# RWKV-7 time mixing in chunks: masks, sums of squares and the order of TensorE rearranged

## The reference

```python
kk = heads(k * p['k_k'])
kk = kk / jnp.maximum(jnp.sqrt(jnp.sum(kk * kk, axis=-1, keepdims=True)), 1e-12)
def step(S, inp):
    r_t, w_t, k_t, v_t, kk_t, b_t = inp            # b = kk * a
    sa = jnp.einsum('bhvk,bhk->bhv', S, -kk_t)
    S = (S * w_t[:, :, None, :] + sa[..., None] * b_t[:, :, None, :]
         + v_t[..., None] * k_t[:, :, None, :])
    o = jnp.einsum('bhvk,bhk->bhv', S, r_t)
    return S, o
mu = jnp.mean(o, axis=-1, keepdims=True)
var = jnp.mean(jnp.square(o - mu), axis=-1, keepdims=True)
o = ((o - mu) * lax.rsqrt(var + LNX_EPS)).reshape(B, L, W) * p['lnx_w'] + p['lnx_b']
```

## Time and profile before

| | |
|---|---|
| median of 3 runs | 2921.92 us (2918.57 to 2924.86) |
| the profiled execution | 2917.37 us |
| its span, first to last instruction | 2915.5 us |
| mean granted clock of TensorE | 0.936 of full |
| RWKV stage, first load to last output | about 1267 to 1793 us |
| a full turn in it (mean of six) | 59.4 us |

### The profile page before, as it was taken

The page is one execution under the profiler, slowest core; times in us unless marked ns, Lnnn a source line. Parts: engine busy times, 40 slices in busy tenths (PEclk is TensorE's granted clock), DMA queues, the critical chain, the costliest instruction groups (busy, mean ns, idle before and its releaser), DMA issues. The chain is left out here.

```text
span 2915.5 us, 48363 instructions
## 1 busy us (share of the span) xinstructions
PE 2679.0 (92%) x20914; PEld 2596.0 (89%) x20914; DVE 1137.0 (39%) x1650; ACT 428.8 (15%) x770; POOL 896.7 (31%) x445
## 2 busy tenths in 40 slices
PE   7999999999899999948899995489989999999997
PEld 7999999999899989947777774379989999999997
DVE  5834826522344554124344442554142122122224
ACT  3100000000200001023444331120031000000011
POOL 3434434343333422300000000154334343434432
PEclk9999999999999999968899886589999999999998
DMA  3111211111334252230001000124111111111111
GB/s 119 42 52 58 74 56 58 54 61 40 109 118 100 81 163 73 90 107 14 18 18 34 6 6 25 51 87 157 61 37 47 47 50 39 49 51 36 58 37 72
DMA packets 81408, 178.88 MB, mean 61 GB/s; under 512 B 11824, under 2 KB 39088, under 8 KB 80128
## 3 DMA queue, kind: packets, MB, share of 16 engines
q1 hardware_dynamic: 59200, 133.65, 14.8%
q10 hardware_dynamic: 22080, 43.36, 4.6%
HBM read 137.48 MB, written 38.33 MB: 60 GB/s over the span
## 5 line engine op out<-in xcount | busy, mean ns | idle before, releaser
L175 POOL TENSOR_TENSOR whi<-wraw,small 128x1024 fp32r<-128x1024 f32 (+3 forms) x214 | 361.3, 1688 | 1331.0 <-PE ps L209 1302.0
L209 PE MATMUL ps<-hhi,whi 128*128 128x344 f32 x3216 | 692.6, 325 | 73.1 <-DVE hhi L2367 24.2
L209 PE MATMUL ps<-hhi,wlo 128*128 128x344 f32 x3168 | 675.0, 322 | 0.0
L209 PE MATMUL ps<-hlo,whi 128*128 128x344 f32 x3120 | 667.2, 322 | 0.0
L209 PEld LDWEIGHTS ps<-hhi,whi 128*128 128x128 f32 x3216 | 547.4, 191 | 77.1 <-issue 55.5
L209 PEld LDWEIGHTS ps<-hhi,wlo 128*128 128x128 f32 x3168 | 534.0, 190 | 0.0
L209 PEld LDWEIGHTS ps<-hlo,whi 128*128 128x128 f32 x3120 | 533.1, 191 | 0.0
L178 POOL TENSOR_TENSOR wlo<-wraw,whi 128x1024 fp32r<-128x1024 f32 (+3 forms) x214 | 506.7, 2368 | 16.8
L209 PE MATMUL ps<-ahi,whi 128*128 128x344 f32 x1056 | 223.9, 320 | 0.0
L209 PE MATMUL ps<-alo,whi 128*128 128x344 f32 x1056 | 223.6, 320 | 0.0
L209 PE MATMUL ps<-ahi,wlo 128*128 128x344 f32 x1056 | 223.1, 319 | 0.0
(11 more groups left out here) (403 smaller groups left out, 2687.8 us busy)
## 6 DMA issues: line engine op xcount, KB each, us to landing
wraw<-ffn_up SPq DMA_DIRECT2D x88, 512.0 KB, 3.5
wraw<-ffn_down SPq DMA_DIRECT2D x32, 384.0 KB, 3.1
wraw<-ffn_down SPq DMA_DIRECT2D x32, 320.0 KB, 2.8
wraw<-w_mix SPq DMA_DIRECT2D x18, 512.0 KB, 3.6
gates<-gate_out ACTq DMA_DIRECT2D x16, 516.0 KB, 2.7
gates_in<-gates SPq DMA_DIRECT2D x16, 516.0 KB, 4.5
wraw<-w_gates SPq DMA_DIRECT2D x16, 512.0 KB, 3.5
f_mixed<-fmix ACTq DMA_DIRECT2D x14, 516.0 KB, 3.7
```

The source lines that it names most:

```text
L175: pool.tensor_tensor(g.whi[:, s, 0:n], g.wraw[:, s, 0:n], g.zero.to_broadcast([P, n]), ALU.add).then_inc(g.w_hi, 1)
L209: last = pe.matmul(g.ps[:, 3 * bank_set + b, 0:BLK], w[:, s, k * P:(k + 1) * P], x(k, b), start=(k == 0 and first), stop=(k == kt - 1 and ...
```

## The change

Masks become predicated copies (`copy_predicated`: where the mask is nonzero, the value is copied, elsewhere the destination keeps what it has). The destinations are prepared once: `X` gets five buffers, one per level, set to zero, and a new `T0` holds identities, which `first` overwrites in its masked places. The product of the identity in `level_x` goes away. `X` then holds only the part off the diagonal, and VectorE adds each level's product to T (`level_sum`), where ScalarE copied the product before. The signs move: `B` is stored negated, and two copies of ScalarE lose their factor -1. `join` on ScalarE uses a buffer of its own, `XJ`.

The sums of squares are turned round: `sums` multiplies a table of 16 selecting columns (weights 128x16) by the squares as moving data (128 columns), for the keys and the outputs together, eight products into one 16x128 result. VectorE scales it and runs the square root on 16 rows by 128 columns; `turned` and ScalarE's copy go away, and `key_scale` and `out_scale` read VectorE's result.

The order on TensorE and VectorE changes as the diff shows: `sums` stands behind `level_x` 3, `gate` behind `level_t` 2, `decayed` behind level 5, `decay_sum` between the sum of level 1 and the mask of level 2, `norms` between the mask and the sum of level 3. On ScalarE the bias of the bonus moves behind `sa`.

```diff
-    g.X, o = g.at("rw_x", o, [P, 2, 4, N])
+    g.X, o = g.at("rw_x", o, [P, 5, 2, 4, N])
...
-            def level(c, j):
-
-                for n in range(2):
-                    inv["pe"].wait(act, c, f"t{j}{n}")
-                    if j < 5:
-                        ins = act.activation(g.T2[:, n].rearrange("p x a c -> p (x a c)"), g.ps[:, 6 + n, :], ACT.Copy)
-                    else:
-                        act.activation(flat(g.T2[lo, n, 0]), g.ps[lo, 6 + n, 0:4 * N], ACT.Copy)
-                        for r in (lo, hi):
-                            ins = act.activation(g.TTF[r, c % 2, 4 * n:4 * n + 4, r], half(6 + n, 1)[r], ACT.Copy)
-                    q_ev.on(ins, f"t{j}{n}")
...
-            st.did(v.tensor_copy(g.identr[:, :], g.ident[:, :]))
-            st.do(v.tensor_copy(g.eyes[:, :].rearrange("p (a c) -> p a c", a=4),
-                                g.rtab[:, T_IST, 0:N].unsqueeze(1).to_broadcast([P, 4, N])))
+            for j in range(5):
+                st.did(v.memset(g.X[:, j], 0.0))
+            st.do(v.tensor_copy(g.T0[:, :, :, :, :].rearrange("p n x a c -> p (n x a) c"), eye(16)))
...
-            def key_norms(d):
-
-                pre["pe"].wait(v, d, "norms")
-                st.do(v.tensor_scalar(g.rsx[:, 0, 0:8], g.ps[:, 0, 0:8], 1e-24, None, ALU.max))
-                p_ev.mark(v, "norms")
...
-                tt(g.B[:, :, :], EA[:, :, :], EX[:, :, :], ALU.mult)
+                st.do(v.scalar_tensor_tensor(g.B[:, :, :], EA[:, :, :], -1.0, EX[:, :, :], ALU.mult, ALU.mult))
...
-                    tt(g.T2[:, n], g.ps[:, 6 + n, :].rearrange("p (x a c) -> p x a c", x=2, a=4), mask0, ALU.mult)
-                    t = g.T2[:, n].rearrange("p x a c -> p (x a) c")
-                    tt(t, t, eye8, ALU.add)
+                    st.do(v.copy_predicated(g.T0[:, n], mask0,
+                                            g.ps[:, 6 + n, :].rearrange("p (x a c) -> p x a c", x=2, a=4)))
                     q_ev.mark(v, f"m{n}")
 
             def level(c, j):
                 for n in range(2):
                     inv["pe"].wait(v, c, f"x{j}{n}")
-                    tt(g.X[:, n], half(4 + n, 0), mask(j), ALU.mult)
+                    st.do(v.copy_predicated(g.X[:, j - 1, n], mask(j), half(4 + n, 0)))
                     q_ev.mark(v, f"x{j}{n}")
+
+            def level_sum(c, j):
+                T = g.T0 if j == 1 else g.T2
+                for n in range(2):
+                    inv["pe"].wait(v, c, f"t{j}{n}")
+                    if j < 5:
+                        tt(g.T2[:, n].rearrange("p x a c -> p (x a) c"), T[:, n].rearrange("p x a c -> p (x a) c"),
+                           bank(6 + n, 8), ALU.add)
+                    else:
+                        tt(g.T2[lo, n, 0], g.T2[lo, n, 0], half(6 + n, 0)[lo], ALU.add, False)
+                        for r in (lo, hi):
+                            tt(g.TTF[r, c % 2, 4 * n:4 * n + 4, r], g.T2[r, n, 1], half(6 + n, 1)[r], ALU.add, r is hi)
+                    q_ev.mark(v, f"t{j}{n}")
...
-            def norms(k, s, p):
+            def norms(k):
                 x, y, t = (g.rsx[:, a, :] for a in range(3))
-                if s is not None:
-                    out["pe"].wait(v, s, "var")
-                    st.do(v.tensor_scalar(x[:, 8:16], g.ps[:, 3, 0:8], 1.0 / N, LNX_EPS, ALU.mult, ALU.add))
+                norm["pe"].wait(v, k, "sums")
+                st.do(v.tensor_scalar(x, g.ps[0:16, 3, CH:2 * CH], g.seg[0:16, 3:4], g.seg[0:16, 4:5], ALU.mult, ALU.add))
+                st.do(v.tensor_scalar(x, x, 1e-24, None, ALU.max))
                 rsqrt_steps(v, st, y, x, t)
                 n_ev.mark(v, "rs")
...
                     gated(y)
                 if q is not None:
-                    scores(q, 0)
-                    scores(q, 1)
-                if p is not None:
-                    key_norms(p)
-                if q is not None:
-                    scores(q, 2)
-                    scores(q, 3)
+                    for n in range(4):
+                        scores(q, n)
                     first(q)
                     level(q, 1)
                 if s is not None:
                     advance(s)
+                if q is not None:
+                    level_sum(q, 1)
                 if p is not None:
                     decay_sum(p)
                 if q is not None:
                     level(q, 2)
+                    level_sum(q, 2)
+                    level(q, 3)
                 if s is not None or p is not None:
-                    norms(k, s, p)
+                    norms(k)
                 if q is not None:
-                    level(q, 3)
+                    level_sum(q, 3)
                 if p is not None:
                     key(p)
                 if q is not None:
                     level(q, 4)
+                    level_sum(q, 4)
+                if p is not None:
+                    key_norm(p)
+                if q is not None:
+                    level(q, 5)
+                    level_sum(q, 5)
                 if p is not None:
                     decayed(p)
-                if q is not None:
-                    level(q, 5)
                 if s is not None:
...
             def level_x(c, j):
+                T = g.T0 if j == 1 else g.T2
                 for n in range(2):
-                    pe.matmul(g.ps[:, 4 + n, 0:4 * N], g.identr[:, :], g.eyes[:, :], start=True, stop=False)
                     if j == 1:
                         inv["dve"].wait(pe, c, f"m{n}")
                     else:
-                        inv["act"].wait(pe, c, f"t{j - 1}{n}")
+                        inv["dve"].wait(pe, c, f"t{j - 1}{n}")
                     for p in range(4):
                         for r in (lo, hi):
                             last = pe.matmul(g.ps[r, 4 + n, p * N:(p + 1) * N], g.SC[r, c % 2, 4 * n + p, 1, 0, r],
-                                             g.T2[r, n, 0, p, :], start=False, stop=p == 3)
+                                             T[r, n, 0, p, :], start=True, stop=True)
                     q_ev.on(last, f"x{j}{n}")
...
-            def var(i):
-                out["act"].wait(pe, i, "sq")
+            def sums(k, i, d):
+
+                use = []
+                if d is not None:
+                    pre["act"].wait(pe, d, "sq")
+                    use += [(p, SQ[:, p, :]) for p in range(4)]
+                if i is not None:
+                    out["act"].wait(pe, i, "sq")
+                    use += [(4 + p, g.osq[:, p, :]) for p in range(4)]
+                for n, (w, x) in enumerate(use):
+                    last = pe.matmul(g.ps[0:16, 3, CH:2 * CH], g.rtab[:, T_SUM, 16 * w:16 * w + 16], x,
+                                     start=n == 0, stop=n == len(use) - 1)
+                n_ev.on(last, "sums")
+
+            def out_scale(k, i):
...
                     tok(q)
                 if s is not None:
                     r0(s)
-                if p is not None:
-                    key_norms(p)
                 if q is not None:
                     scores(q, 0)
                     scores(q, 1)
@@ -1964,33 +1952,32 @@
                     o(s)
                 if q is not None:
                     level_x(q, 1)
-                if s is not None:
-                    centre(s)
                 if p is not None:
                     lora(p, 1)
                 if q is not None:
                     level_t(q, 1)
+                if s is not None:
+                    centre(s)
+                if q is not None:
                     level_x(q, 2)
+                    level_t(q, 2)
                 if p is not None:
                     gate(p)
-                if s is not None:
-                    var(s)
-                if q is not None:
-                    level_t(q, 2)
-                if s is not None or p is not None:
-                    turned(k)
                 if q is not None:
                     level_x(q, 3)
+                if s is not None or p is not None:
+                    sums(k, s, p)
+                if q is not None:
+                    level_t(q, 3)
+                    level_x(q, 4)
                 if p is not None:
                     key_scale(k, p)
                 if q is not None:
-                    level_t(q, 3)
+                    level_t(q, 4)
+                    level_x(q, 5)
                 if s is not None:
                     out_scale(k, s)
                 if q is not None:
-                    level_x(q, 4)
-                    level_t(q, 4)
-                    level_x(q, 5)
                     level_t(q, 5)
                     join(q)
```

129 lines of the change are left out of this document (57 added, 72 removed).

## The result

The changed kernel takes 2901.73 us (median of 4 runs, 2898.35 to 2906.01), the kernel before 2923.39 us beside it (4 runs, 2918.57 to 2926.18): ratio 0.9928, 95% interval 0.9909 to 0.9948. It is 0.7% or about 21 us faster. The forecast was 2925 us, slower or the same; the range began at 2904.

A forecast was written before the change was run, and what follows sets the result against it. TensorE, busy for 92% of the span, was taken as the bound, with its waits and half-clock time. Full turns 7 x -0.2, first turn +4.7 and last +0.9 gave +4 us on the 2921.92 median: about 2925 us, range 2904 to 2942.

The forecast's parts named there:

- The walk through the queues: Stepping through TensorE's and VectorE's queues in one full turn: new waits of 7.6 us against 4.75 before.
- The chain: VectorE's square root on 16x128: thirteen instructions, 3.9 us in place of 2.45, bounds 2.7 and 4.2.
- the first turn: Stage's first turn, where nothing hides `norms`: `tok` at 1308.2 in place of 1303.54, 4.7 us later.
- the rival that it reads twice: Predicated copies on VectorE take 0.69 and 1.22 us, masks stand open at every level: +5, 2930 us; chance 0.10.
- 10 x 0.31 = 3.1 us: TensorE time saved per full turn by dropping ten identity products in the levels, 0.31 us each.
- seven turns: The sum over the stage multiplied the per-turn change of -0.2 us by 7.
- The step on the clock: Change in a turn's half-clock loss: 0.5 us less at the moved stretch, 0 to 1.7 more around `join` and `tok`.
- 0.5 us less lost: Half-clock stretch moves from behind `gate` to behind the wait before `level_x` 4, covering 0.8 us of small waits.
- 0 to 1.7 us more lost: Longer idle around `join` and `tok` costs up to half of one more 3.4 us half-clock stretch per turn.
- the half-clock stretch goes with the wait: No clock fall follows the wait before `level_x` 4, or it is nearer 1.7 us: 2904 us; chance 0.27.

The follow-up runs named there:

- old_norms: Kernel after with the sums of squares and square root put back to 128 rows by 16 columns, in their new place; ratio 0.9881 to the kernel before.
- no_eye_gate_late: Kernel before without the identity products, `gate` and `var` behind `level_t` 2 and `turned` behind `level_x` 3; 2887.7 us, ratio 0.9887.
- r0_old_norms: Kernel after with queues reordered (`sums` behind `level_t` 2, `bonus` before `join`, `r0` before `tok`) and square root back in 128x16; 2864.1 us, ratio 0.9807.
- split_norms: Kernel after with the square root cut in two on VectorE around sum 3 and level 4's masks, `key_scale` behind `level_t` 4; 2909.4 us, ratio 0.9950.

## Why the prediction was wrong

**The walk through the queues held.** It stepped through each engine's queue in order. Waits forecast and found, in us: 1.0 and 1.09 before `level_t` 2, 2.9 and 2.94 before `level_x` 4, 1.1 and 0.43 + 0.67 in `join`, 0.8 and 0.61 before `tok`, none before `gate`. The chain was 3.9 and 3.97 us; the first turn +4.7 and +4.4. The predicated copy takes 442 ns for a forecast 0.42 us, so the rival that it reads twice is out; of 128x512 it takes 735 ns. VectorE's add took 687 ns as its row said. The stage's last turn came out 0.6 us shorter where 0.9 longer was forecast.

**The term "10 x 0.31 = 3.1 us" was mis-sized.** By the pitch of the blocks a product costs 0.38 us: 0.31 to the next start and 0.07 in the products behind it. That is 0.7 us per turn. `sums` took 1.85 us for a forecast 2.1 to 2.2, another 0.25. The waits rise by 2.55 us at full clock, by the estimate in the next paragraph, where 2.85 were forecast. Together that is 1.2 us per turn at full clock, 7 us in six turns. The prediction counted seven turns, although it says itself that the turn without a new chunk comes out even, and it did (+0.1); six is the right number, here and below.

**The step on the clock failed in its sign.** "0.5 us less lost", then "0 to 1.7 us more lost" around `join` and `tok`, came to some 0.1 us more. In the profiled pair the full turns have 2.3 us less at half clock each (72 us for 85 in six turns), where half the work is done, so up to 1.1 us less is lost. A sum says the same. For the turn without any half clock the kernel with one Newton step has rows: 50.87 us, and with the six instructions that it leaves out (1.87 us) 52.7 for the kernel after, with 7.5 us of waits. For the kernel before I estimate TensorE's 45.25 us of that row, ten products at 0.38, 0.25 for the sums, and 4.94 us of waits (57.42 less 52.48 in the earlier trace rows), which make 54.2. So at full clock the change is worth 1.5 us per turn (forecast 0.3). The turns measured are 59.4 and 56.75: the half clock costs 5.2 us before and 4.0 after, 1.1 less. Against the forecast that is 1.2 us per turn, 7 us in six, as much as the error at full clock.

The split between the two is not sharp. The 4.94 us is read in a turn in which half clock hides VectorE's chain behind `level_t` 2. Without it `turned` would wait too, by 0.6 us or so as I estimate from the 0.81 us in old_norms, and that much moves from the clock's part to that at full clock. And the clock's part rests on one execution of each kernel.

The rival "the half-clock stretch goes with the wait" had the nearest time (2904), but not for its reason: the 2.94 us wait has its half-clock stretch in each of the six turns.

**The rest is between executions.** The profiled pair differs by 11.4 us, the medians by 21.7. Of the four executions of the kernel after the profiled one is the slowest and has the lowest granted clock of the whole span (0.937; the others 0.938, 0.938, 0.941). Such differences between executions, 7.7 us over these four, are as large as either error above, so how much of the remaining 10 us is chance isn't known, and part of the clock's error may be chance too.

**What each part was worth.** Identity products and order together 33 us faster (no_eye_gate_late). The square root in 16 rows cost 14 (old_norms). That leaves a cost of 2 us for everything else, with VectorE's adds and the predicated copies in it, which are what lets the identity products go. This adds up runs on two different kernels, each good to some 7 us, and these parts don't add exactly (29 and 17 gave 33). So that the adds and copies are about even in themselves is inferred, not shown; no run has them alone.

**What stays open** is what makes the clock fall. A longer single wait makes it fall for longer (20, 72 and 95 us at half clock in six turns with one, three and five steps). But less waiting in all does not keep it up: 5.6 us of waits per turn in the kernel with one step go with full clock, 2.7 in r0_old_norms with two falls in most turns, and old_norms waits 16 us less than after and has 10 us more at half clock. Neither the number of waits nor the run of 64x64 products explained it. The Trainium skill ("TensorE: Matmul & The Clock Gate", "HAM oscillation") puts the fall down to idle stretches between bursts, in its example longer ones than any of the kernel after; the three Newton kernels agree, split_norms, old_norms and r0_old_norms show that the idle time alone doesn't rank kernels.

## What to carry to other kernels

Price a removed product by the pitch of the whole block with and without it, not by the distance to the next start, and then walk through the queues again: here waits took back 8.7 of 22.8 us. Keep a chain of dependent VectorE instructions in the layout with the fewest columns per row, and look at what is queued behind it: 1.3 us of chain cost 14 us over nine turns, 1.87 us cost 33 or 34. Where the clock of a stage moves between its two levels, a sum at full clock gives only half of the answer; try orders on the chip, several at a time, and don't expect that fewer or shorter waits rank them.
